# Turning the weights of seven differential heads with DMA transposes instead of TensorE, and shifting the steps of each pair's second head

## The reference

```
s1 = q1 @ k1.T * scale + bias          # 256 x 256
s2 = q2 @ k2.T * scale + bias
p  = softmax(s1) - lam * softmax(s2)   # 256 queries x 256 keys
o  = p @ v                             # 256 x 128
y  = rms_norm(o, subln) * (1 - lambda_init) * silu(gate)
```

## Time and profile before

| what | value |
|---|---|
| median of 3 runs | 3057.98 us (3057.90 to 3058.08) |
| the profiled execution | 3058.66 us |
| its span, first to last instruction | 3056.9 us |
| PE busy | 3043.0 us, 100% |
| DVE busy | 1869.1 us, 61% |
| ACT busy | 1469.8 us, 48% |
| POOL busy | 134.2 us, 4% |
| chain that ended last | PE 97%, DVE 1%, ACT 1%, DMA 1% |

### The profile page before, as it was taken

One profiled execution on the slowest core, in us unless ns is written; L12 is line 12 of the kernel. 1 busy time (PEld: TensorE's weight loads), 2 busy tenths in 40 slices (PEclk: granted clock), 3 DMA queues, 4 the chain that ended last, 5 costly groups with the idle time before them and its releaser, 6 DMA issues.

```text
span 3056.9 us, 48305 instructions
## 1 busy us (share of the span) xinstructions
PE 3043.0 (100%) x20906; PEld 2827.8 (93%) x20906; DVE 1869.1 (61%) x2263; ACT 1469.8 (48%) x1699; POOL 134.2 (4%) x132
## 2 busy tenths in 40 slices
PE   9999999999999999999999999999999999999999
PEld 9989999999999999989888888889998889999987
DVE  7775555445445557776565565556787666767663
ACT  5544433333333357755443443345565654555553
POOL 0001000000000011110000000002000001101000
PEclk9999999999999999999999999999999999999999
DMA  6334555555554554455555555554444545555554
GB/s 236 108 111 166 174 173 178 179 177 171 176 179 168 182 195 176 159 193 179 194 191 188 185 179 198 187 192 179 179 140 153 178 175 184 179 193 186 174 191 152
DMA packets 94516, 539.57 MB, mean 177 GB/s; under 512 B 25568, under 2 KB 26080, under 8 KB 31584
## 3 DMA queue, kind: packets, MB, share of 16 engines
q1 hardware_dynamic: 77264, 532.14, 50.0%
q10 hardware_dynamic: 17040, 4.34, 0.8%
HBM read 530.15 MB, written 2.10 MB: 174 GB/s over the span
## 4 chain that ended last, share of the span: by engine, by line
PE 97%; DVE 1%; ACT 1%; DMA 1%; issue 0%; SPq 0%; ACTq 0%; DVEq 0%
PE PB L1158 28%; PE PB L1159 15%; PE PB L1183 14%; PE PB L1182 14%; PE PB L1184 13%; PE PB L1177 2%; PE PB L1178 2%; PE PB L1179 2%; PE PB L1169 1%; PE PB L1168 1%; PE PB L1167 1%; PE PB L1240 1%; DMA raw<-in_mla_in 1%; PE PB L1308 1%; DVE WLt L1796 0%; PE PB L1309 0%
## 5 line engine op out<-in xcount | busy, mean ns | idle before, releaser
L1796 DVE TENSOR_TENSOR WLt<-raw,WHt 128x2048 fp32r<-128x2048 f32 (+2 forms) x506 | 1139.3, 2259 | 760.7 <-ACT WHt L1415 760.2
L1415 ACT ACTIVATE WHt<-raw 128x2048 fp32r<-128x2048 f32 (+2 forms) x506 | 955.0, 1890 | 1117.3 <-PE PB L1159 582.0
L1158 PE MATMUL PB<-Xt,WHt 128*128 128x512 f32 x2880 | 1027.6, 395 | 0.0
L1159 PE MATMUL PB<-Xt,WLt 128*128 128x256 f32 x2880 | 808.5, 281 | 0.0
L1158 PEld LDWEIGHTS PB<-Xt,WHt 128*128 128x128 f32 x2880 | 540.8, 188 | 109.8
L1182 PE MATMUL PB<-Xt,WHt 128*128 128x272 f32 (+1 forms) x2192 | 635.0, 290 | 2.8 <-DVE WLt L1796 1.9
L1183 PE MATMUL PB<-Xt,WHt 128*128 128x272 f32 (+1 forms) x2192 | 630.2, 287 | 0.0
L1184 PE MATMUL PB<-Xt,WLt 128*128 128x272 f32 (+1 forms) x2192 | 626.9, 286 | 0.0
L1159 PEld LDWEIGHTS PB<-Xt,WLt 128*128 128x128 f32 x2880 | 543.5, 189 | 0.1
L1182 PEld LDWEIGHTS PB<-Xt,WHt 128*128 128x128 f32 x2192 | 412.8, 188 | 12.6 <-DVE WLt L1796 4.9
L1183 PEld LDWEIGHTS PB<-Xt,WHt 128*128 128x128 f32 x2192 | 413.5, 189 | 1.1 <-issue 0.2
(11 more groups left out here) (268 smaller groups left out, 2858.1 us busy)
## 6 DMA issues: line engine op xcount, KB each, us to landing
raw<-in_gu SPq DMA_DIRECT2D x176, 1024.0 KB, 4.8
raw<-in_dn SPq DMA_DIRECT2D x88, 1024.0 KB, 4.8
raw<-in_odd_in SPq DMA_DIRECT2D x64, 1024.0 KB, 4.8
raw<-in_even_in SPq DMA_DIRECT2D x52, 1024.0 KB, 4.9
raw<-in_lru_in SPq DMA_DIRECT2D x24, 1024.0 KB, 4.9
raw<-in_mla_o SPq DMA_DIRECT2D x16, 1024.0 KB, 4.8
raw<-in_lru_o SPq DMA_DIRECT2D x16, 1024.0 KB, 5.0
raw<-in_even_o SPq DMA_DIRECT2D x16, 1024.0 KB, 4.9
```

The source lines that it names most:

```text
L1158: t.matmul(o, wh, both, start=first, stop=False)
L1159: m = t.matmul(o[:, 0, :], wl, ah, start=False, stop=last)
L1415: a.activation(hi, r, ACT.Copy).then_inc(s_hi, 1)
L1796: v.tensor_tensor(lo, r, hi.bitcast(f32), sub).then_inc(s_lo, 1)
```

## The change

For the differential heads 8 to 14, `t_` (PE transposes and a copy from PSUM) is replaced by two steps. `x_` copies `E1` on ACT into two planes of 16-bit halves in the buffer `sqt` and issues a DMA transpose from ACT into `acct`. `w_` weaves the halves back, one on ACT and one on DVE. Head 15 keeps `t_`. For pairs 0 to 2 the steps of the second head and what follows it move: `v_(1)`, the squares and `n1_` from after F1 to after F2, and `n2_` from after F2 to after F3. For pair 3 their places stay.

```diff
+        def x_(j):
+            hd = ("e", 8 + 2 * q + j)
+            p.mark("diff planes", "diff planes", hd)
+            p.step("diff_planes", hd)
+            now["E1"] = ("diff planes", hd)
+
+        def w_(j):
+            hd = ("e", 8 + 2 * q + j)
+            p.mark("diff woven", "diff woven", hd, 1)
+            p.mark("diff woven low", "diff woven", hd, 0)
+            p.step("diff_weave", hd, bufs[j], now[bufs[j]])
...
-            p.step("weigh_rows", hd, "Vp", j, bufs[j], cur["v"])
+            turned = [("out", "tr", hd)] if hd[1] == 15 else [("diff woven", hd, i) for i in range(2)]
+            p.step("weigh_rows", hd, "Vp", j, bufs[j], turned, cur["v"])
...
         if q < 3:
-            return {0: lambda: s_(0), 2: lambda: (t_(0), s_(1)), 4: lambda: (t_(1), v_(0)),
-                    5: lambda: (v_(1), q_(), n1_()), 6: n2_}
+            return {0: lambda: s_(0), 2: lambda: (x_(0), s_(1)), 3: lambda: w_(0), 4: lambda: (x_(1), v_(0)),
+                    5: lambda: w_(1), 6: lambda: (v_(1), q_(), n1_()), 7: n2_}
         p.mid = lambda: (v_(1), q_())
-        return {0: lambda: s_(0), 2: lambda: (t_(0), s_(1)), 4: lambda: (t_(1), v_(0)), 5: n1_, 6: n2_}
+        return {0: lambda: s_(0), 2: lambda: (x_(0), s_(1)), 3: lambda: w_(0), 4: lambda: (t_(1), v_(0)), 5: n1_, 6: n2_}
...
+        DIFF_PLANES, DIFF_CROSSED = sqt[:, 0:512], acct[:, 0:512]
...
+            def diff_planes(hd):
+                n = hd[1] - 8
+                a.wait_ge(*when("pp", hd))
+                if n:
+                    a.wait_ge(s_diff_crossed, 16 * n)
+                    for i in range(2):
+                        a.wait_ge(*when("diff woven", ("e", hd[1] - 1), i))
+                a.activation(DIFF_PLANES.bitcast(u16).rearrange("p (a n) -> p a n", a=2), halfwords(E1),
+                             ACT.Copy).then_inc(sems["diff planes"], 1)
+                a.wait_ge(*when("diff planes", hd))
+                x = DIFF_CROSSED.bitcast(u16).rearrange("p (g n) -> p g n", n=128)
+                a.dma_start(x, DIFF_PLANES.bitcast(u16), transpose=True).then_inc(s_diff_crossed, 16)
...
+            def diff_weave(hd, b, free):
+                a.wait_ge(s_diff_crossed, 16 * (hd[1] - 7))
+                if free:
+                    a.wait_ge(*when(*free))
+                a.activation(half_words(buf[b], 1), plane(DIFF_CROSSED, 1), ACT.Copy).then_inc(sems["diff woven"], 1)
...
+            def diff_weave(hd, b, free):
+                v.wait_ge(s_diff_crossed, 16 * (hd[1] - 7))
+                if free:
+                    v.wait_ge(*when(*free))
+                low = DIFF_CROSSED.bitcast(u16)[:, 0:512].rearrange("p (q k n) -> p k q n", q=2, k=2)
+                v.tensor_copy(buf[b].bitcast(u16).rearrange("p (k q n a) -> p a k q n", k=2, q=2, a=2)[:, 0],
+                              low).then_inc(sems["diff woven low"], 1)
```

More of the change, by code:

```diff
@@ L1029, in build_program @@
             ctx.enter_context(nc.semaphore(f"s_{n}")) for n in ("par", "cst", "lams", "tabA", "tabB", "last_gain", "out"))
+        s_diff_crossed = ctx.enter_context(nc.semaphore("s_diff_crossed"))
         s_crossed = ctx.enter_context(nc.semaphore("s_crossed"))
@@ L1331, in turn, with weigh_rows @@
                 m.then_inc(sems["tr"], 1)
-            def weigh_rows(hd, V, vj, b, vready):
+            def weigh_rows(hd, V, vj, b, turned, vready):
                 bank = own("pv", hd)
-                t.wait_ge(*when("out", "tr", hd))
+                for ready in turned:
+                    t.wait_ge(*when(*ready))
                 t.wait_ge(*when(*vready))
@@ L1614, in turn_split, with plane, half_words @@
                 a.activation(TTH, PB[bk][:, :], ACT.Copy).then_inc(sems["trh"], 1)
+            def diff_planes(hd):
[10 more added lines that the diff above has]
+                a.dma_start(x, DIFF_PLANES.bitcast(u16), transpose=True).then_inc(s_diff_crossed, 16)
+            def plane(x, i):
+                return x.bitcast(u16)[:, 512 * i:512 * i + 512].rearrange("p (q k n) -> p k q n", q=2, k=2)
+            def half_words(x, i):
+                return x.bitcast(u16).rearrange("p (k q n a) -> p a k q n", k=2, q=2, a=2)[:, i]
+            def diff_weave(hd, b, free):
[3 more added lines that the diff above has]
+                a.activation(half_words(buf[b], 1), plane(DIFF_CROSSED, 1), ACT.Copy).then_inc(sems["diff woven"], 1)
             def crossed(hd):
@@ L1733, in _ @@
                     crossed(*x)
+                elif what == "diff_planes":
+                    diff_planes(*x)
+                elif what == "diff_weave":
+                    diff_weave(*x)
                 elif what == "uq_out":
```

## The result

| | before | after |
|---|---|---|
| median | 3058.03 us (3057.9 to 3058.4, 4 runs) | 3090.76 us (3087.89 to 3091.59, 4 runs) |
| profiled execution, span | 3058.66, 3056.9 | 3091.35, 3089.6 |
| ratio | | 1.0106, 95% interval 1.0093 to 1.0118 |

The kernel became 32.7 us slower. The forecast was 3064.0 and its range ended at 3067.5, so the result lies outside it. The loss is in the stage of the pairs, and the page alone already says where to look. First the page of the changed kernel: busy times, PE by slices, the chain by engine and line, and the transposes' issues.

What follows compares the result with a forecast made beforehand. PE, busy practically the whole span, was taken to bound the kernel. Savings less waits gave +1.58 us in pair 0, +1.18 each in pairs 1 and 2, +2.06 in pair 3: 3057.98 + 6.0 = 3064.0 us, range 3058.5 to 3067.5.

Steps and rivals of the forecast that it cites:

- A landing takes 2.7, at worst 6.5 us: Time for a DMA transpose to land in the pairs' stage, so ACT stands just ahead of the copies before `vv_out`.
- Nothing, or 0.2 at worst: PE's wait at `v_(1)` for the second head's weave, its step moved a unit later: none, or 0.2 us.
- SP's loads keep more than 2 us of slack: SyncE's weight loads in the pairs' stage would keep more than 2 us of slack.
- The planes: ACT's copy of `E1` into two halfword planes: 1.23 us, bounds 1.02 and 1.57, making DVE's chain 1.66 us late.
- `v_(0)`: PE waits there for DVE's weave behind `split_low`: 1.13 us in pair 0, 0.73 in pairs 1 and 2.
- G0's bank: PE waits at G0's fourth tile until `o_norm` has read `turn_out`'s PSUM bank: 1.32 us, pairs 0 to 2.
- the sign against its main argument: No gap in PE's rows around `v_(0)` and in G0 would show the main argument wrong.
- Pair 3: In the output projection's second unit, `v_(1)` waits for ACT's copy of head 15: +2.06 us.
- Everything hidden: Rival: PE never waits in the pairs' stage, so the change saves its 3.1 us, 3054.9 us; chance 0.13.
- No wait at the bank: Rival: in G0 `o_norm` reads in time or another bank comes fourth; 3 x 1.32 go, 3060.0 us; chance 0.10.
- The longer issue: Rival: the DMA issue holds ACT 2.26 us, making the exponentials late, +3.1 us, 3067.1 us; chance 0.10.
- The whole duration as a price: Rival: each PE transpose costs its full 0.272 us, so 7.6 us saved, 3050.4 us with nothing waiting; chance 0.02.

Runs made afterwards that it cites:

- experiment 1: Changed kernel, with SyncE holding back the weight load behind each second head's DMA transpose until that has landed; 3063.95 us, ratio 1.002.
- experiment 4: Changed kernel, with all seven transposes issued by SyncE in the queue of the loads instead of by ACT; 3063.59 us, ratio 1.0018.
- experiment 5: Changed kernel, with the load 1.2 us ahead of each second head's transpose cut to 16 of its 2048 columns; 3064.64 us, ratio 1.0022.
- experiment 6: Changed kernel, with the load 1.4 us behind each second head's transpose cut to 16 of its 2048 columns; 3064.85 us, ratio 1.0022.
- experiment 2: Kernel before, PE transposes kept, only `v_(1)`, squares and `n1_` moved after F2 and `n2_` after F3, pairs 0 to 2; 3062.41 us, ratio 1.0013.
- experiment 11: Kernel of experiment 4 with planes and weaves at other places, `v_(1)` and `n2_` back (pair 3's `v_(1)` later), second head's planes on GpSimd; 3057.39 us.
- experiment 8: Changed kernel, ACT still issuing, planes a unit sooner, `v_(1)` and `n2_` at old places, pair 3's `v_(1)` one block later; 3074.14 us, ratio 1.0054.
- experiment 7: Changed kernel, SyncE issuing, planes a unit sooner, `v_(1)` and `n2_` at old places, pair 3's `v_(1)` one block later; 3076.64 us, ratio 1.0062.
- experiment 3: Changed kernel, but only first heads turned by DMA; second heads on PE and other steps at their old places; 3060.62 us, ratio 1.0008.
- experiment 9: Kernel of experiment 4, with DVE's `split_low` behind `o_norm` instead of ahead after F3 of pairs 0 to 2; 3062.61 us, ratio 1.0014.
- experiment 12: Kernel of experiment 11, with the wait for the first head's weaves on SyncE and DVE's weave ahead of `split_low`; 3060.91 us, ratio 1.0009.

## Why the prediction was wrong

**The failed step** is "A landing takes 2.7, at worst 6.5 us", and what was built on it for the second head: "Nothing, or 0.2 at worst". 2.7 to 6.5 were the landings of the odd layer, and I carried them over as the property of the operation. They are landings among other transfers. In fifteen of the odd layer's sixteen the last load is 4.1 to 5.7 us old when the transpose is issued; the sixteenth, with one 0.9 us old, landed after 5.6 us. Here one is 1.2 us old and the next comes 1.4 us behind. The measured landings are 12.8 and more, where the walk had room for 6.5. The same rows warned: a maximum 2.4 times the median, for the same bytes, says that something outside the transfer sets its time. The neighbours don't explain all of it either: the 6.5 us landing had its loads 5.7 us ahead and 1.4 behind, as seven others that took 2.7 to 2.8. I wrote "SP's loads keep more than 2 us of slack" and looked only at whether the loads were late, not at what they do to the transpose. Experiments 1, 4, 5 and 6 take the step's cause away in four ways and give 3063.6 to 3064.9.

The Trainium skill (DMA: Bandwidth & Descriptors, "Rules for kernel authors") says that transfers of several issuing engines run on the same 16 DMA engines and interleave. The trace agrees that they share, since the load behind crawls too (12.7 us). But at the 281 GB/s of the kernel before the transpose and that load, 1.31 MB together, would be through in 4.7 us, an estimate from that row, and not in 12.8; the rule gives no sign of the standstill, and the measurement decides.

**The clock** behind the stalls was in no term either, 7.5 us, and 1.7 behind pair 3's. The first follows from the long stalls and goes with them. Experiment 1 then lands on the forecast, 3063.95 against 3064.0, and so close a hit is luck: against the kernel before timed beside it, it is 5.7 above where 6.0 was forecast, and its profiled execution, the slowest of ten, is 7.2 above, with pairs 0 to 2 at 4.3 instead of 3.94, pair 3 at 1.8 instead of 2.06 and the 1.7 of clock that the sum lacks.

**The planes** took 1.04 us (1.034 to 1.042, seven times), not my 1.23: near the lower bound. The Trainium skill (ScalarE: Activation LUTs, "What ACT_TABLE_LOAD costs") was right here with 1.04, and wrong for the interleaving write of 512 halfwords, where the trace after has 0.78 again and the rule 0.61. A read with stride and a write with stride aren't the same kind; I took the wrong row. It moved `L2233`'s counterpart 0.19 less, and no term by more than 0.2. (Its 0.87 ns for an element should be 0.85: 1.31 us over 1536. That changes 0.01 us.)

**`v_(0)`** was forecast at 1.13, 0.73, 0.73 and came as 1.13 (1.25 less 0.12), 0.99, 0.58. In pair 0 that is exact, and the releaser is the one named, DVE's weave. In pairs 1 and 2 the sum is 1.57 against 1.46.

**G0's bank**: 1.32 forecast, 1.24 in experiments 1, 2 and 4. My reading of `take` and `give` is shown by the releaser, DVE's L2299 and its counterparts. In the changed kernel itself the wait is absent, which the prediction named as the sign against its main argument; there the lower clock between `v_(1)` and G0 hid it.

**Pair 3**: 2.06 forecast; from its `s_(0)` to its `v_(1)` the changed kernel lost 1.8, as did experiment 1 (3.8 late at 2461.65, 5.6 late at 2491.62).

**The rivals.** "Everything hidden" fell: experiment 1 has waits at both places in each of pairs 0 to 2. "No wait at the bank" looked right in the changed kernel and fell in experiment 2. The longer issue fell: six of the seven took 1.25 to 1.33 us and one 1.87, where it needed 2.26 each time. The whole duration as a price fell: up to pair 3 experiment 1 has waits of 2.7 at `v_(0)` and 3.7 in G0 and 24 transposes less. At 0.44 and 0.43 for four that makes +3.8, at 0.272 each -0.2, and it came 4.3 later.

**Left open**: why both loads are needed. The runs show that, at these distances, it needs a load ahead, one behind and a second issuer, and that the loads' packets then hang for up to 6.9 us, not what happens inside the queues. At which distances it begins is open too: 1.2 and 1.4 us gave 12.8 and more, 1.73 and 1.71 gave 4.4, the only such case. Whether 3057.4 can be bettered is open too: experiment 11's remaining waits are 1.24, 1.98 and 1.06 us, and the one attempt on them failed.

## What to carry to other kernels

A landing time belongs to the traffic around it: before carrying it over, list for each new transfer the last load ahead and the next one behind, and take the rows with the same neighbours at the same distances; if there are none, the bound is open upwards, and even the same neighbours gave 2.7 or 6.5 us here. In this kernel it helped to put the transfer that the critical engine needs into the queue of the large loads, or to hold the load behind it. And moving PE's own work to a chain ACT, DMA, ACT and DVE saves only what it takes from start to start, 0.43 us a turn, against every wait in three queues: at best it came out even here.

## What the runs showed of the hardware

A DMA transpose of 128 x 1024 halfwords issued by ACT landed after 12.8 to 15.5 us between two 1 MB loads of SyncE (1.2 us ahead, 1.4 us behind), three times in three; after 3.1 with the load ahead cut, 4.8 to 5.2 with the one behind cut, 4.8 to 6.1 with that one held, and 4.6 to 4.8 from SyncE's own queue. The load behind it took 12.7 to 15.3 instead of 4.8 to 5.4. With the loads 1.73 ahead and 1.71 behind it landed after 4.4 (experiment 8).

After stalls of 6.6 to 9.3 us PE's granted clock averaged 0.66 to 0.77 over the following 7 to 9 us, after two of 2.95 and 2.36 in experiment 7 0.62 and 0.57 over 4 us, and after one of 2.96 there 1.00. The same stall of 2.1 us in pair 3, with the work before it alike, was followed by a stretch at 1.2 GHz in the profiled executions of the changed kernel and of experiments 1, 3, 5 and 9, and by none in those of 4 and 6. These windows of 1 and then 4 show it. So a wait of 2 us can cost 1.7 more, and the same wait nothing.

```profile
2492.00:2497.00 5.00, 5.00 (x24) 4.40 (x23) 1.53 (x2) 1.67 (x9) 0.00 (x0) 0.66 0.94 367
```

```profile
2492.00:2497.00 5.00, 5.00 (x32) 4.47 (x32) 1.56 (x2) 1.66 (x9) 0.00 (x0) 1.00 0.88 360
```

GpSimd's copy of 128 x 1024 halfwords and DVE's `split_low` side by side cost the one that starts later. In experiment 12 the copy began 0.2 us ahead, three times in three: it took 1.21 us instead of the 1.04 of 11, and `split_low` 3.14 instead of 2.28. In the odd layer `split_low` began 0.15 ahead, eight times in eight: it took 2.28, and the copy 3.03. The first of these in the kernel before:

```profile
2610.31 2.28 DVE L1796 TENSOR_TENSOR WLt<-raw,WHt 128x2048 fp32r<-128x2048 f32 x1
...
2610.46 3.03 POOL L2486 COPY S<-S 128x1024 uint16<-128x1024 uint16 x1 [35.00 <-DVE S L2255]
```

The Trainium skill (GPSIMD Engine Reference, "1. Specifications") says that the two engines share their SBUF interfaces when the DVE instruction has two SBUF inputs, as this one has: the trace agrees, and shows what it costs.
